# A two-layer mixture trunk: one program for both layers' expert retrieval, with the recurrent mixer beside the gathers

## The reference

```python
for l in range(DEPTH):
    ...
    h = _rmsnorm(x, p['norm1_g'][l]) * (1 + sc1) + sh1
    y = even or odd mixer(h)                 # y = (hf + flip(hb)) * gelu(gate) @ w_out in the odd one
    x = x + g1 * y
    h = _rmsnorm(x, p['norm2_g'][l]) * (1 + sc2) + sh2
    x = x + g2 * _peer(h, ...)

# _peer, for every block of 128 tokens
q = (xb @ w_q).reshape(PEER_BLOCK, PEER_HEADS, 2, PEER_DK // 2)
v1, i1 = lax.top_k(s1, PEER_TOPK)            # s1, s2: scores of the two halves against 128 keys
v2, i2 = lax.top_k(s2, PEER_TOPK)
sc, pos = lax.top_k(cand, PEER_TOPK)         # 16 of the 256 sums
g = jax.nn.softmax(sc, axis=-1)
act = jax.nn.gelu(jnp.einsum('thkd,td->thk', u[eidx], xb))
out = jnp.einsum('thk,thkd->td', (g * act), v[eidx])

# _odd_mixer: centred convolution of width 4, then, forward and backward in time
r, i = sigmoid(block-diagonal products of the convolved x)
a = exp(-8 * softplus(-lam) * r);  h_t = a_t h_{t-1} + sqrt(1 - a_t^2) (i_t x_t)
```

## Time and profile before

| what | us |
|---|---|
| three timed executions | 4525.49, 4538.74, 4539.86 |
| their median | 4538.74 |
| the profiled execution | 4535.62 |
| its span, first to last instruction | 4533.8 |

### The profile page before, as it was taken

One profiled execution on the slowest core, in us unless ns is written; L12 is line 12 of the kernel. 1 busy time (PEld: TensorE's weight loads), 2 busy tenths in 40 slices (PEclk: granted clock), 3 DMA queues, 4 the chain that ended last, 5 costly groups with the idle time before them and its releaser, 6 DMA issues. The chain is left out here.

```text
span 4533.8 us, 54616 instructions
## 1 busy us (share of the span) xinstructions
PE 3131.9 (69%) x15503; PEld 1210.7 (27%) x15503; DVE 3204.4 (71%) x7667; ACT 1156.9 (26%) x2563; POOL 1468.5 (32%) x1316
## 2 busy tenths in 40 slices
PE   7698888766576766666655997767575666666655
PEld 2266564312121211112111553312121211112111
DVE  6633343778787878888887354778787878877886
ACT  4432141222222222221223341222222222221222
POOL 0000000344344444444443000344344444444443
PEclk9899968878786778778777998878686877787777
DMA  8510003999999999999997113999999999999998
GB/s 319 194 48 29 34 0 124 374 420 392 413 406 392 418 399 421 390 420 398 421 412 315 70 37 120 372 420 392 406 402 399 418 389 421 395 421 388 421 411 336
DMA packets 207051, 1468.87 MB, mean 324 GB/s; under 512 B 24281, under 2 KB 29161, under 8 KB 35689
## 3 DMA queue, kind: packets, MB, share of 16 engines
q0 software_dynamic: 184320, 1342.26, 72.2%
q1 hardware_dynamic: 21684, 121.29, 7.0%
q10 hardware_dynamic: 828, 2.76, 0.2%
HBM read 1462.84 MB, written 3.38 MB: 323 GB/s over the span
## 5 line engine op out<-in xcount | busy, mean ns | idle before, releaser
L802 PE MATMUL peer_acc<-peer_ring,peer_diag 64*64 64x512 f32 x10240 | 1749.6, 790 | 1125.9 <-DVE peer_diag L666 1122.1
L439 POOL DMA_INDIRECT peer_ring<-in_uv,peer_index x1280 | 1456.1, 1138 | 2494.4 <-PE peer_acc L802 1668.8
L658 DVE CUSTOM_DVE_ANT_0 peer_ring<-peer_ring,HY 128x1024 f32<-128x1024 f32 x1280 | 1561.8, 1221 | 398.7 <-DMA peer_ring<-in_uv,peer_index 311.1
L802 PEld LDWEIGHTS peer_acc<-peer_ring,peer_diag 64*64 64x64 f32 x10240 | 392.9, 160 | 2202.7 <-issue 2170.8
L521 ACT ACTIVATE peer_acts<-peer_dots 128x1 f32<-128x1 f32 x1280 | 258.6, 203 | 2498.6 <-DVE peer_dots L658 2497.9
L666 DVE TENSOR_SCALAR peer_diag<-ident,peer_acts,peer_gate 128x128 f32<-128x128 f32 x1280 | 439.1, 343 | 15.9 <-ACT peer_acts L521 14.5
L753 PE MATMUL peer_qp<-HT,peer_wq 128*128 128x512 f32 (+1 forms) x896 | 366.6, 539 | 0.0
L753 PEld LDWEIGHTS peer_qp<-HT,peer_wq 128*128 128x128 f32 x896 | 180.6, 224 | 373.8 <-issue 367.3
L501 ACT ACTIVATE peer_tmp<-peer_acc 64x512 f32<-64x512 f32 x320 | 189.0, 591 | 53.4 <-PE peer_acc L802 49.8
L672 DVE TENSOR_TENSOR peer_tmp<-peer_tmp,peer_G 128x1024 f32<-128x1024 f32 x80 | 98.0, 1225 | 89.9 <-ACT peer_tmp L501 83.4
L717 PE MATMUL peer_acc<-peer_ring,HY 128*128 128x512 f32 x320 | 144.6, 614 | 14.8 <-DMA peer_ring<-in_w_out 14.8
(11 more groups left out here) (281 smaller groups left out, 2973.1 us busy)
## 6 DMA issues: line engine op xcount, KB each, us to landing
mod_wmod<-in_w_mod SPq DMA_DIRECT2D x16, 2048.0 KB, 9.8
peer_ring<-in_uv,peer_index POOLq DMA_INDIRECT x1280, 16.3
HT<-in_w_mod SPq DMA_DIRECT2D x8, 2048.0 KB, 9.6
peer_wq<-in_w_q SPq DMA_DIRECT2D x16, 1024.0 KB, 11.7
peer_ring<-in_w_out SPq DMA_DIRECT2D x8, 1024.0 KB, 8.3
lru_wlru<-in_w_lru SPq DMA_DIRECT2D x4, 2048.0 KB, 8.4
hgrn_wqvg<-in_w_hgrn_qvg SPq DMA_DIRECT2D x4, 1536.0 KB, 6.7
peer_ring<-scratch_mod_rows SPq DMA_DIRECT2D x12, 512.0 KB, 13.7
```

Source lines behind the costliest of these rows:

```text
L439: pool.indirect_dma_start(ring[:, j % SLOTS, :], None, uv[:, :], bass.IndirectOffsetOnAxis(ap=index[:, j:j + 1], axis=0), element_offset=l ...
L658: dve.tensor_tensor_reduce(u, u, H[:, j // TOPK, :], 1.0, 0.0, ALU.mult, ALU.add, dots[:, j:j + 1]).then_inc(dot_done, 1)
L802: last_mm = pe.matmul(acc[b % 2][c * HALF:(c + 1) * HALF, r * 512:(r + 1) * 512], diag[rows, j % NDIAG, rows], ring[rows, j % SLOTS, D + c ...
```

## The change

Both calls of `project_and_peer` and `rglru` are replaced by one program, `trunk`, that is written out without hardware loops.

- Order of units: in each layer first the sample's 32 units (head by head, four tiles), then the prompt's 8. The sample's part of the recurrent mixer is spread over layer 0's prompt units (slots 521 to 633, from `SAMPLE` = 512), and the prompt's part over heads 1 to 4 of the sample's units in layer 1. `big` and `small` are its working buffers: `big` is cut out of ring slots 6 to 9, `small` out of slot 9.
- The ring has ten slots, but `ring_slots` lets only six be used by the first 64 slots of each layer and by layer 0's 128 prompt slots, and nine by the next 320 slots of layer 1.
- `background()` on PE, DVE and ACT is a generator. It yields the number of the slot after which its next piece is put out. The projection and norm of the later tiles, the queries and the recurrent mixer are such pieces, so a layer's gathers start when one tile is normalised.
- The prompt's units of a layer add up in one PSUM accumulator over all 8 heads and are added to X once (`ends_sum`).
- SP loads all weights in pieces of 1 MB into two buffers, in the order in which PE uses them (`pieces`). The mixer's `w_lru` and `w_rg` are loaded twice, once for each stream.
- `made_by_act` is false for every slot, so DVE makes every diagonal, as L666 does in the kernel before.

```diff
-SLOTS = 10
...
-def project_and_peer(nc, X, H, HT, ident, iota16, layer, io):
...
-                        if j == FREE:
-                            pool.wait_ge(projected, NB)
-                        if j == NORM:
-                            pool.wait_ge(h_ready, NB)
-                        if j % TOPK == 0:
-                            pool.wait_ge(index_ready, h * NB + (j // TOPK + 1))
-                        wait_apart(pool, slot_free, h * PER_HEAD + (j + 1))
-                        pool.indirect_dma_start(ring[:, j % SLOTS, :], None, uv[:, :],
-                                                bass.IndirectOffsetOnAxis(ap=index[:, j:j + 1], axis=0),
-                                                element_offset=layer * EXPERTS * 2 * D)\
-                            .then_inc(landed[j % SLOTS], 16)
...
-                def head(h, last):
-                    r = None
-                    for j in range(PER_HEAD):
-                        b, s = divmod(j, TOPK)
-                        dot(h, j)
-                        if j:
-                            weight(h, j - 1)
-                        nb = next_unit(b, last)
-                        unit = h * NB + (b + 1)
-                        if nb is not None:
-                            if s == 1:
-                                r = route_a(unit)
-                            if s == 3:
-                                route_b(r)
-                            if s == 5:
-                                route_c(r, nb)
-                            if s == 7:
-                                route_d(r, unit, nb)
-                        if s == 7 and b:
-                            add_unit(h, b - 1)
-                        if last and s == 12 and b:
-                            norm(NB + b - 1)
...
+RING = 10
+SMALL = 6
+UNITS = LAYERS * HEADS * NB
+SLOTS_IN_ALL = UNITS * TOPK
+SPAN = HEADS * NB * TOPK
+SAMPLE = HEADS * SB * TOPK
...
+def made_by_act(g):
+    return False
+def ring_slots():
+    last, fills, table = {s: None for s in range(RING)}, [0] * RING, []
+    for g in range(SLOTS_IN_ALL):
+        if g < SB * TOPK or SAMPLE <= g < SPAN + SB * TOPK:
+            allowed = range(SMALL)
+        elif SPAN <= g < SPAN + 6 * SB * TOPK:
+            allowed = range(RING - 1)
+        else:
+            allowed = range(RING)
+        slot = min(allowed, key=lambda s: (-1 if last[s] is None else last[s], s))
+        table.append((slot, fills[slot], last[slot]))
+        last[slot], fills[slot] = g, fills[slot] + 1
+def route_steps(u):
+    return (2, 4, 6, 8, 10) if u % (HEADS * NB) < SB else (0, 1, 3, 5, 7)
+def end_steps(u):
+    return (1, 3, 4, 6, 7, 8) if u == HEADS * SB else (3, 7, 9, 12, 14, 15)
+def trunk(nc, X, HY, HT, ident, iota16, io):
...
+        pieces = [("q", 0, h) for h in range(HEADS)]
+        pieces += [(part, n, 0) for n in range(RB) for part in ("xr", "gt", "rg")]
+        pieces += [("q", 1, 0), ("q", 1, 1)]
+        for h in range(1, HEADS - 1):
+            pieces.append(("q", 1, h + 1))
+            if h <= RB:
+                pieces += [(part, h - 1, 1) for part in ("xr", "gt", "rg")]
+            elif h == RB + 1:
+                pieces += [("out", i, 1) for i in range(4)] + [("qp", 1, 0)]
+            else:
+                pieces += [("qp", 1, i) for i in range(1, 5)]
+        pieces += [("qp", 1, i) for i in range(5, HEADS)]
...
+                for g in range(SLOTS_IN_ALL):
+                    u, s = divmod(g, TOPK)
+                    slot, fills, before = table[g]
+                    if s == 0:
+                        pool.wait_ge(index_ready, u + 1)
+                    if g == INTERVAL:
+                        pool.wait_ge(projected, NB)
+                    if g == SPAN + INTERVAL:
+                        pool.wait_ge(projected, NB + SB)
+                    if g == SPAN + 6 * INTERVAL:
+                        pool.wait_ge(l_y, 2 * KD)
+                    if before is not None:
+                        pool.wait_ge(slot_free, before + 1)
+                    pool.indirect_dma_start(ring[:, slot, :], None, uv[:, :],
+                                            bass.IndirectOffsetOnAxis(ap=index[:, u % 2, s:s + 1], axis=0),
+                                            element_offset=unit_of(u)[0] * EXPERTS * 2 * D)\
+                        .then_inc(landed[slot], 16)
+
...
+                    sample_lru = lru(lambda n, what: SAMPLE + 9 + 24 * n + {"xp": (9, 10), "gt": (18, 19), "sig": (22, 27),
+                                                                          "ex": (23, 32), "sq": (27, 36)}[what[0]][what[1]], 0)
+                    yield from with_prompt_keys(sample_lru)
...
+                    yield from lru(lambda n, what: SAMPLE + 9 + 24 * n + {"conv": (12, 13), "mix": (25, 34), "scan": (29, 38),
+                                                                         "y": (31, 40)}[what[0]][what[1]], 0)
+                    yield SPAN - 3
+                    residual(5, qp)
+                    yield SPAN - 1
+                    norm(5)
+                    r = route_a(HEADS * NB)
+                    route_b(r)
+                    route_c(r, HEADS * NB)
+                    route_d(r, HEADS * NB)
+                    residual(6, qp)
+                    norm(6)
+                    yield SPAN + 6
+                    residual(7, qp)
+                    yield SPAN + 8
...
+                for g in range(SLOTS_IN_ALL):
+                    u, s = divmod(g, TOPK)
+                    dot(g)
+                    if g and g != SPAN:
+                        weight(g - 1)
+                    if g == SPAN - 1:
+                        weight(g)
+                    if u + 1 < UNITS and (u + 1) % (HEADS * NB):
+                        steps = route_steps(u)
+                        if s == steps[1]:
+                            r = route_a(u + 1)
+                        if s == steps[2]:
+                            route_b(r)
+                        if s == steps[3]:
+                            route_c(r, u + 1)
+                        if s == steps[4]:
+                            route_d(r, u + 1)
+                    if s == end_steps(u)[1] and u and ends_sum(u - 1):
+                        add_sum(u - 1)
+                    if s == end_steps(u)[3] and u and ends_tile(u - 1) and ends_sum(u - 1):
+                        end_norm(unit_of(u - 1)[0] * NB + unit_of(u - 1)[2])
+                    while due is not None and due <= g:
...
+                    yield from lru(lambda n, what: SAMPLE + 9 + 24 * n + {"xr": (0, 4), "gt": (8, 12), "rg": (16, 20)}[what[0]][what[1]], 0)
+                    for k in range(KD):
+                        yield SPAN - 13 + k
+                        pe.wait_ge(l_evac, 12 * RB)
+                        pe.wait_ge(w1_in[k], 16)
+                        if k >= 6:
+                            pe.wait_ge(l_y, KD)
+                        project(5, qp, [k], resident)
...
+                for g in range(SLOTS_IN_ALL):
+                    u, s = divmod(g, TOPK)
+                    nxt = u + 1 if u + 1 < UNITS and (u + 1) % (HEADS * NB) else None
+                    if nxt is not None and s == route_steps(u)[0] == 0:
+                        scores(nxt)
+                    accumulate(g)
+                    if nxt is not None and s == route_steps(u)[0] > 0:
+                        scores(nxt)
+                    if s == end_steps(u)[4] and u and ends_tile(u - 1) and ends_sum(u - 1) and unit_of(u - 1)[0] == 0:
+                        end_turn(unit_of(u - 1)[2])
+                    while due is not None and due <= g:
+                        due = next(rest, None)
+
+    phase(nc, "trunk", body)
```

1650 lines of the change are left out of this document (1073 added, 577 removed).

## The result

The changed kernel takes 4403.66 us (median of four runs, 4397.87 to 4408.68); the kernel before, on the same chip, 4536.57. The ratio is 0.9711 with a 95% interval of 0.969 to 0.9732: 133 us or 2.9% less. The forecast was 4290 with 4180 to 4440. The direction and the range were right, but the gain is about half of what was forecast, and the time lies above the forecast's own range (4210 to 4370).

A forecast was written before the change was run, and what follows sets the result against it. The prediction took the kernel as a DMA-paced stream of 1280 gathers with a 382.3 us hole between the layers. Eight steps and 18 us at the end sum to 4285, adjusted to 4290 us, range 4180 to 4440.

The forecast's parts named there:

- Step 1: Start of the kernel to the first dot: at 765 us, where it was 815.11 before.
- Step 5: Last dot of layer 0 to first of layer 1: 40 us, bounds 27 and 60, where it was 382.3.
- step 3: Slots 64 to 511, ring of ten, nothing at head ends: 2.55 us a slot, 1142 us.
- step 7: Layer 1's 320 slots with the prompt's mixer: 816 us, 47 for 20 MB, 10 for PE's waits, 873 us.
- step 8: Last 256 slots: 128 at 2.55 us, 10 us for 4 MB, 128 at 2.5, together 656 us.
- Steps 2 and 6: First 64 slots of each layer, six ring slots: 2.9 us a slot, 186 us each.
- Step 4: Layer 0's 128 prompt slots, six ring slots: 96 at 3.5 us beside the sample's mixer, 32 at 2.6, 419 us.
- A: Mixer hides well: step 4 at its floor of 2.85, step 7's bytes hidden, starts at 2.6: 4143 us; chance 0.19.
- B: In step 4 PE's clock falls to its lower level, 96 slots at 5.15 us: 4448 us; chance 0.14.
- C: Each ACT table switch costs a good 2.6 us and DVE feels it: 4356 us; chance 0.04.
- D: Straight code stalls on instruction loading, slower than before: 100 stalls of 4.69 us give 4759 us; chance 0.05.
- E: No difference: gains of steps 1, 3 and 5 all given back in 2, 4, 6 and 7; chance 0.02.

The follow-up runs named there:

- e2: Changed kernel loading only an eighth of layer 1's pieces for the prompt's mixer, output weights and queries, 21 MB less: 4338.37 us, ratio 0.9577.
- e12: Changed kernel with 24 small DVE operations, a hole of 11 us, at the start of 14 of the sample's heads: 4448.46 us, ratio 0.9821.
- e1: Changed kernel with the gate products of layer 1's prompt mixer six slots later on PE, what follows shifted too: 4392.04 us, ratio 0.9697.
- e3: Changed kernel with only six ring slots allowed in all 1280 slots: 4560.83 us, ratio 1.0060 to the kernel before.
- e9: Changed kernel with five ring slots instead of six in the stretches that use six: 4435.16 us, ratio 0.9799.
- e11: Changed kernel with gate products later and the fuller ring given back sooner, all work done: 4375.52 us, ratio 0.9658.
- e5: Changed kernel with DVE's operations cut to 32 of 512 columns in three of four parts of the sample's mixer: 4372.79 us, ratio 0.9649.
- e6: Changed kernel with ACT's operations except sigmoids cut to 32 of 512 columns in three of four sample's mixer parts: 4392.06 us, ratio 0.9701.
- e8: Changed kernel with ACT using the gelu's function for the sample's mixer, so its table loads go: 4387.88 us, ratio 0.9687.
- e7: Changed kernel with PE's mixer products cut to 32 of 512 columns in three of four parts of the sample's mixer: 4402.15 us, ratio 0.9715.
- e4: Changed kernel with the sample's mixer in one piece behind slot 626 instead of spread over slots 521 to 633: 4489.21 us, ratio 0.9907.

## Why the prediction was right, and where it was too low

**Step 1** was right as reasoned: a chain of serial work that can be added up from its rows. The first residual started at 721.3 instead of 725.5, the routing ended at 753.3 for 758, and the first dot waited 5.45 us for its gather.

**Step 5** has the right number by luck. 25 us of chain and 15 for late weight rows make 40, and 39.2 were measured, but the wait for the weight rows isn't there: PE stood 4.3 us in all for `w_out`, and that before the last dot. Two other terms filled its place. The chain up to the first issue took 26.3 us (2572.18 to 2598.44) and not 25.3 - 6.5 = 18.8. And DVE's order has the residual and the norm of the next tile ahead of the first dot, which starts at 2611.34 without a wait for its gather:

```profile
2598.44 0.94 POOL L1222 DMA_INDIRECT trunk_ring<-in_uv,trunk_index  x1 [34.23 <-DVE trunk_index L1668]
...
2603.24 1.23 DVE L1587 TENSOR_TENSOR HY<-trunk_qp,trunk_G 128x1024 f32<-128x1024 f32 x1 [4.72 <-PE trunk_qp L1915]
...
2608.68 0.16 DVE L1595 RECIPROCAL trunk_rs<-trunk_rt 128x1 f32<-128x1 f32 x1 [2.96 <-ACT trunk_rt L1249]
```

**Steps 3, 7 and 8: bytes left out.** These are 63 of the 118 us. The pace of 2.55 came from the last turn of the loop, which loads no query weights; the prediction called its difference to the other heads the head's end. In the changed kernel each head of 64 slots loads 1 MB of them, and step 3 puts them at nothing. The queues of the changed kernel from slot 64 to 511 (964 to 2133) have 11.0 MB beside the gathers:

```profile
q0 software_dynamic: 64712, 471.26, 98.0%
q1 hardware_dynamic: 2944, 8.39, 1.8%
q10 hardware_dynamic: 1584, 2.62, 0.6%
```

At 421 GB/s these are 26 us, and the step missed by 27. Likewise step 7 has 20 MB and the trace 23.6 (8 us of its 17), and step 8 has 4 MB and the trace 10.8 (16 us of its 20). This is an estimate: that such bytes are paid in full was measured by e2, in step 7's stage alone, and no run takes layer 0's query weights away. The 2.55 itself stands as the pace of the gathers alone: (1168.6 - 26) / 448 = 2.55, and 2.56 in e2. A hole of the head's end's length on DVE, to which the prediction gave the difference, is worth half a us in layer 0 by e12.

**Step 7's other terms.** 47 us for 20 MB and 10 for waits. e2 measures some 37 for its 15.6 MB and e1 11 for the waits: both terms hold. The mixer's weights are loaded once more than before, because the two streams use them at different times.

**Steps 2 and 6, 2.9 a slot.** Measured 3.2. I added each engine's work and took the largest sum. By e3 six slots cost 0.14 a slot with no extra work at all, by e9 a slot less 0.1 to 0.2 more, and e11 gave 0.3 back in the part of layer 1 where nine could be had. No experiment took the projection apart, so which lump makes the 0.45 beyond the bare ring is open. The term that was too low is the pace of 2.9; the runs show 0.14 a slot for the ring in it and leave the rest open.

**Step 4, 3.5 and 2.6.** Measured 3.46 over all 127 slots, 3.56 from 528 to 623. The mechanism was the right one: e5, e6 and e8 each gain a part and none all, so the pace belongs to lumps on several engines under a small ring; PE's own part e7 leaves open. My sum was low at its edges, 2.6 a slot for 32 slots: slots 512 to 527 cost 3.0, those behind 623 cost 3.3, and even without a mixer beside them six slots cost 2.73 (e4).

**The rivals.** A, all at its floor, didn't come: the bytes are paid (e2) and the window's pace is 3.5, not 2.85. B needed a fallen clock in the window; it was 0.92, with PE busier than any other engine, which was the reason given against B. e7 shows 0.65 when PE has less to do. C is out by e8. D: between the first dot and the last DVE has no wait for "issue" among its waits of the changed kernel and PE none above 1.2 us, and the instruction queues moved about what they did before, 226 packets for 219:

```profile
q8 instruction: 111, 1.82, 0.2%
q14 instruction: 115, 0.94, 0.1%
```

E had the right thought, gains that are given back inside the layers (269 of 399 us), but a third of the gain stayed.

**The signs it named.** Between the gathers of slots 64 to 511 POOL's longest gap is 4.75 us; in the heads before it was 13. The window took 439 us at a clock of 0.92, with a DMA share of 0.91 where under 0.9 was named. Layer 1's heads with the mixer moved 397 GB/s and not 424. The last 256 slots ran at 676.1 / 255 = 2.65, just at the mark it had set for being wrong.
